# The cubic of a GELU gate: from two GpSimd operations to a scaled square and one VectorE operation

## The chip, the cores and the metric

The kernel runs on one core of a Trainium2 chip. Its time is device microseconds of one launch, and the median of a few runs is compared. The profile is that of one execution, with a clock that starts at its first instruction.

A core has a matrix engine (TensorE, PE), and three engines that work on tiles of 128 partitions: VectorE (DVE), ScalarE (ACT) and GpSimd (POOL). SyncE (SP) issues most of the transfers. Each engine takes its instructions in the order in which they are written, and the engines wait for each other through semaphores.

## The reference

Two layers of a streaming encoder over 16 meta tokens, 1024 prompt tokens and 32 sample tokens, 1024 wide. In each layer a normalised input is multiplied by one combined matrix, whose columns are the low-rank query, the latent of keys and values, the rotary key, the input of a linear recurrence, and the recurrence's gate:

```python
z = rmsnorm(x, norm_mix_g) @ w_in
c_q, c_kv, k_r, x_r, g_r = jnp.split(z, IN_SPLITS, axis=-1)
...
_, h = lax.associative_scan(lru_combine, (a, b), axis=1)
y = h.astype(x.dtype) * jax.nn.gelu(g_r)
```

`jax.nn.gelu` is the tanh form: 0.5 g (1 + tanh(sqrt(2/pi) (g + 0.044715 g^3))). Attention, an output projection and a squared-ReLU MLP follow. Everything is in float32, on 512 gate channels per layer.

## The kernel before, in words

Activations lie transposed: features on the 128 partitions, tokens in the free dimension (1074 columns with two of padding; in the second layer the gate needs only 1056). The 512 channels of recurrence and gate are four tiles, c = 0 to 3, called channels below. All engines' programs are written out by hand in one fixed order each, and all waits are explicit.

**Exact products by splitting.** Every float32 product is three passes on PE: high part times high part, high times low, low times high (`product`, line 975 of the profile; the rotary key's two passes are line 1099). The weights of block b are loaded by SP into `raw_all`, ACT rounds them to `whi` (`split` in ACT's program, L1551), DVE subtracts to give `wlo` (`split` in DVE's, L2294; `split_kr`, L2306, for the rotary key). Both are two buffers deep. ACT's split of block b waits until PE has finished block b-2. PE waits for `w_hi` before the first pass of a product and for `w_lo` before the third; the gates and the rotary-key product wait for `w_lo` at their first.

**PE's order in this stage:** four recurrence inputs, gate products 0 and 1 (blocks 4 and 5), recurrence gates of channel 0 (block 6, a short unit: L1033 and L1036), gate products 2 and 3 (7, 8), recurrence gates 1 (9), latent (CKV) products 0 and 1 (10, 11), recurrence gates 2 (12), rotary key (13), query products 0 and 1 (14, 15), recurrence gates 3 (16), the remaining query products (17 to 20).

**PSUM.** Two slots of three banks hold the products in turn. DVE's `scaled` (L2317) empties a slot into SBUF, multiplied by the inverse root of the mean square. PE reuses a slot only after that.

**The gate's path for channel c.** `gelu_a` on ACT squares `g[c]` into the tile `t2` (L1610, semaphore `g_sq`). `cube` on POOL turns it into the cubic in two operations (L3267 and L3269, semaphore `g_cube`). `gelu_b` on ACT takes the tanh (L1614, `g_tanh`). `gelu` on DVE makes the product with the recurrence's state (L2375, L2376, `y`).

**The recurrence's path.** ACT's `gate_r`, `gate_i`, `decay` and `normal` lead to DVE's `lru` (three operations L2360, L2362, L2363, then the scan L2365). `xc_hi` on ACT and `xc_lo` on DVE make the input of the recurrence gates.

**The orders around the change.** ACT: for channel 0 `normal(0)`, `split(9)`, `gelu_a(0)`, `gelu_b(0)`, `split(10)`, `gate_r(1)`; for channel 1 `normal(1)`, `split(12)`, `gelu_a(1)`, `gelu_b(1)`, `split(13)`, `gate_r(2)`; for channel 2 `gelu_a(2)`, `split(16)`, `gelu_b(2)`, squares of the latent, `split(17)`; for channel 3 `gelu_a(3)`, `split(19)`, inverse root of the latent, `gelu_b(3)`. DVE's order is in the diff.

Of the kernel before, what the change touches and what calls it, by code (L numbers as in the profile page):

```python
# [15 lines left out]
ALU = mybir.AluOpType  # L16
ACT = mybir.ActivationFunctionType
# [19 lines left out]
LAST_KEYS, SAMPLE_KEYS = 8 * P, 9 * P  # L37
assert SAMPLE_KEYS == PAST_A + PAST - 48 and LAST_KEYS + 64 == PAST_A + NMETA and KEY_END == SAMPLE_KEYS + 112
GELU_C = float(np.sqrt(2.0 / np.pi))


B_XR, B_GR, B_CKV, B_KR = [0, 1, 2, 3], [4, 5, 7, 8], [10, 11], 13
# [39 lines left out]
def pairs(name, j):  # L82
    return groups(name, NGROUP) + PAIR[name] * (j - NPAIR + 1) if j else 0
# [334 lines left out]
def trunk(nc, xT, wst, vec, fgain, ropeC, ropeS, ident_in, past_ckv, past_kpe, h0, conv0,  # L418
          yT, ckv_out, kpe_out, h_out, conv_out, x_scr, sum_scr):
    ctx = ExitStack()  # L420
    with ctx:
# [14 lines left out]
        def place(name, region, offset, cols, dt=F32):  # L436
            return nc.alloc_sbuf_tensor_at(name, [P, cols], dt, offset=regions[region] + offset, align_bytes=8)

        def tiles(name, region, first, n, dt=F32):
            return [place(f"{name}{i}", region, (first + i) * TB, T, dt) for i in range(n)]  # L440
# [11 lines left out]
        t1, t2, t3 = (tp[i][:, 0:T] for i in range(3))  # L452
        t4 = tp[3]
        xr = [tp[3], tp[0], tp[1], tp[2]]
        g = tiles("g", "G", 0, 4)
        ckv = [place(f"ckv{i}", "CK", i * KB, KW) for i in range(2)]
        kpe = place("kpe", "KP", 0, KW)
# [85 lines left out]
        def sb(name, shape, dt=F32):  # L543
            return enter(nc.sbuf_tensor(name, shape, dt))
# [4 lines left out]
        sp2, spw = sb("sp2", [P, 4]), sb("spw", [P, 16])  # L549
# [17 lines left out]
        def sem(name, per_layer=0):  # L567
            s = enter(nc.semaphore(name))
            PER[name] = per_layer
            S[name] = s  # L570

        S = {}
        for name, per in (
            ("dve_chain", DVE_CHAIN), *ALL_RAW.items(), ("w_hi", B_MLP), ("w_lo", B_MLP), ("mm", NU),
            ("sum", 6), ("vec_in", 16), ("small_in", 48), ("table_in", 32), ("const_in", 0), ("const_set", 0), ("head_in", 0), ("head", 0), ("ones_set", 0),
            *((f"x_in{m}", 32) for m in range(8)), ("x_out", 32 * 8), *((f"staged{i}", 0) for i in range(N_STAGE)), ("xg_hi", 8), ("xg_lo", 8), ("sq", 8), ("sq_sum", 7),
            ("root", 6), ("rstd", 6), ("sum_hi", 4), ("sum_lo", 4),
            ("xr_ev", 4), ("xr_raw", 0), ("conv", 4), ("xc_hi", 4), ("xc_lo", 4),
            ("gate_r", 4), ("gate_y", 4), ("gate_t", 4), ("gate_i", 4), ("root_t", 4), ("hid", 4),
            ("gr_ev", 4), ("g_sq", 4), ("g_cube", 4), ("g_tanh", 4), ("y", 4),  # L580
            ("ckv_ev", 2), ("ckv_sq", 2), ("ckv_sum", 1), ("ckv_n", 2), ("ckv_hi", 2), ("ckv_lo", 2),
            ("kr_lo", 1), ("kr_ev", 1), ("kpe", 16 * 4), ("kpe_copy", 1), ("kpe_ones", 1), ("kv_out", 32), ("ckv_full", 1), ("hid_out", 1), ("small_out", 48), ("g_poly", 4), ("spw_abs", 1), ("spw_exp", 1), ("sp2", 1),
            ("cq_ev", 6), ("cq_sq", 6), ("cq_sum", 5), ("cq_hi", 6), ("cq_lo", 6),
            ("qr_raw", 2), ("qn", 4), ("qr", 2), ("ra0", 16 * 4), ("ra1", 16 * 4),
            ("y_sq", 4), ("y_sum", 3), ("y_n", 4), ("v_one", 1), ("v_ev", 10), ("kf", 4),
            ("kslot_hi", 3), ("kslot_lo", 4),
            ("slot1_set", 2 + NH // 2 - 1), ("p_zero", 5), ("qn_hi", NH), ("q_hi", NH), ("k_hi", NH), ("q_lo", NH), ("s", NH * NP), ("p", NH * NP),
            ("pv", NH * NP), ("mxmm", NH * NMX), ("mxred", NH * NMX), ("mxc", NH), ("mxt", NH), ("mt_hi", NH), ("mt_lo", NH),
            ("aug", 32 * NH), ("aug_few", 32 * NH), ("o_ev", 3 * NH), ("s_ev", 3 * NH), ("sum_out", 16 * NH), ("sum_in", 16 * 4), ("inv", 4), ("inv_out", 16 * 4),
            ("inv_in", 16 * NH), ("o", 4), ("o_sq", 4), ("o_sum", 3), ("o_hi", 4), ("o_lo", 4),  # L590
            ("y_hi", 4), ("y_lo", 4), ("oy_ev", 8), ("oo_ev", 8), ("xm_f", len(F_ORDER)), ("xm_hi", 24), ("xm_lo", 24), ("xm_sq", 8), ("xm_sum", 7),
            *((name, pairs(name, NPAIR)) for name in ("draw0", "draw1", "s_made", "u_sum", "u_hi", "u_lo", "up", "p_copy", "c_add", "down", "d_add",
                                                      "relu", "f_sq", "f_hi", "f_lo", "prod", "t_made", "x_copy", "x_add", "d_sum")), ("res_add", 8),
            ("end_sq", 0), ("end_sum", 0), ("end_log", 0), ("end_rs", 0),
            ("yout", 0), ("y_st", 0),
        ):
            sem(name, per)
# [913 lines left out]
        def _(act):  # L1511
# [29 lines left out]
            for L in range(DEPTH):  # L1541
                def w(name, k):
                    assert k > 0, name
                    act.wait_ge(S[name], L * PER[name] + k)
# [10 lines left out]
                def live(tile):  # L1555

                    return tile[:, LIVE[0]:LIVE[1]]
# [48 lines left out]
                def gelu_a(c):  # L1606
                    w("gr_ev", c + 1)
                    if c:
                        w("y", c)
                    nc.scalar.activation(live(t2), live(g[c]), ACT.Square).then_inc(S["g_sq"], 1)  # L1610

                def gelu_b(c):
                    w("g_cube", c + 1)
                    nc.scalar.activation(live(t2), live(t2), ACT.Tanh, scale=GELU_C).then_inc(S["g_tanh"], 1)  # L1614

# [209 lines left out]
                for gi in range(NH * NP):  # L1825
# [20 lines left out]
                    if h == NH - 1 and i in Y_AT:  # L1846
                        c = Y_AT.index(i)
# [376 lines left out]
        def _(dve):  # L2224
            V = nc.vector
# [38 lines left out]
            for m in range(8):  # L2264
                dve.wait_ge(S["xg_hi"], m + 1)
                V.scalar_tensor_tensor(out=xgl[m][:, :], in0=x[m], scalar=col(V_GMIX + m), in1=xgh[m][:, :].bitcast(F32),
                                       op0=ALU.mult, op1=ALU.subtract).then_inc(S["xg_lo"], 1)
# [9 lines left out]
            for L in range(DEPTH):  # L2277
# [12 lines left out]
                def split(b):  # L2290

                    w("w_hi", b + 1)
                    n = WCOLS[b]
                    V.tensor_tensor(wlo[b % 2][:, 0:n], raw[b % 2][:, 0:n], whi[b % 2][:, 0:n].bitcast(F32), ALU.subtract).then_inc(S["w_lo"], 1)  # L2294
# [7 lines left out]
                def split_kr():  # L2302

                    w("w_hi", B_KR + 1)
                    hi, src = (t[B_KR % 2][:, :].rearrange("p (k n) -> p k n", k=8)[:, :, 64:P] for t in (whi, raw))
                    V.tensor_tensor(hi, src, hi.bitcast(F32), ALU.subtract).then_inc(S["w_lo"], 1)  # L2306
# [7 lines left out]
                def scaled(u, dst, by, name, at=(0, T)):  # L2314

                    w("mm", u + 1)
                    V.tensor_tensor(chunks(dst, at), slot(u, at), chunks(by, at), ALU.mult).then_inc(S[name], 1)  # L2317
# [38 lines left out]
                def lru(c):  # L2356
# [12 lines left out]
                    V.tensor_copy(hbuf[:, c, 0:1], xc[c][:, STREAM - 1:STREAM])  # L2369
                    link(V.tensor_copy(hbuf[:, c, 1:2], xc[c][:, TOK - 1:TOK]))  # L2370

                def gelu(c):

                    w("g_tanh", c + 1)
                    link(V.scalar_tensor_tensor(out=live(g[c]), in0=live(t2), scalar=1.0, in1=live(g[c]), op0=ALU.add, op1=ALU.mult))  # L2375
                    V.scalar_tensor_tensor(out=live(g[c]), in0=live(g[c]), scalar=0.5, in1=live(xc[c]), op0=ALU.mult, op1=ALU.mult)\  # L2376
                        .then_inc(S["y"], 1)
# [77 lines left out]
                lru(0)  # L2455
                split(9)
                scaled(U_GR[3], g[3], rs, "gr_ev", LIVE)
                split(10)
                gelu(0)
                xc_lo(2)  # L2460
# [2 lines left out]
                lru(1)  # L2463
                split(12)
                scaled(U_CKV[1], ckv[1][:, 0:T], rs, "ckv_ev")
                split_kr()
                gelu(1)
                split(14)
# [4 lines left out]
                split(15)  # L2473
                lru(2)
                split(16)
                scaled(U_CQ[0], cq[0], rs, "cq_ev", LIVE)
                gelu(2)
                scaled(U_CQ[1], cq[1], rs, "cq_ev", LIVE)
# [4 lines left out]
                lru(3)  # L2483
                w("root", SUM_KV)
                scaled(U_CQ[2], cq[2], rs, "cq_ev", LIVE)
                split(19)
                gelu(3)
                V.tensor_copy(hbuf[:, 3, 1:2], xc[3][:, TOK - 1:TOK]).then_inc(S["hid_out"], 1)
# [183 lines left out]
                for h in range(NH):  # L2672
                    for i in range(NP):
# [21 lines left out]
                        if h == NH - 1 and i in Y_AT:  # L2695
                            c = Y_AT.index(i)
# [542 lines left out]
        def _(pool):  # L3239
            G = nc.gpsimd  # L3240
# [4 lines left out]
            for L in range(DEPTH):  # L3245
                def w(name, k):
                    assert k > 0, name
                    pool.wait_ge(S[name], L * PER[name] + k)
# [11 lines left out]
                def live(tile):  # L3260

                    return tile[:, LIVE[0]:LIVE[1]]

                def cube(c):

                    w("g_sq", c + 1)
                    G.tensor_scalar(live(t2), live(t2), 0.044715, 1.0, ALU.mult, ALU.add).then_inc(S["g_poly"], 1)  # L3267
                    w("g_poly", c + 1)
                    G.tensor_tensor(live(t2), live(t2), live(g[c]), ALU.mult).then_inc(S["g_cube"], 1)  # L3269

                def add(acc, tmp, sq, out, m):

                    w(sq, m + 1)
# [7 lines left out]
                def y_add(m):  # L3281
                    add(live(t3), live(t4), "y_sq", "y_sum", m)

                for c in range(3):
                    cube(c)
                sum_squares(ckv_tmp[0][:, :], ckv_tmp[1][:, :], 2, "ckv_sq", "ckv_sum")
                cube(3)
                y_add(1)
                cq_add(1)
                y_add(2)  # L3290
# [280 lines left out]
```

## Time and profile before

| | |
|---|---|
| median of 3 runs | 2461.35 us (2460.33 to 2462.65) |
| profiled execution, span | 2460.3 us |
| PE, DVE busy | 2447.1, 1782.1 us |
| ACT, POOL busy | 1250.7, 517.4 us |
| stage of the gate, first layer | about 73 to 194 us |
| stage of the gate, second layer | about 1300 to 1420 us |

The page gives the profiled execution's own time as its span alone, from the first to the last instruction; the three timed runs are other executions of the same program. A line of the profile names the engine, the source line and the tiles, with the duration and, in brackets, how long the engine sat idle before and who ended that. Consecutive operations of one engine overlap by about 0.1 us, so start-to-start times are a little shorter than durations.

### The profile page before, as it was taken

To read this page: it belongs to the slowest core of one execution; us is meant where nothing else is said; L and a number is where in the kernel's file an instruction comes from. 1 tells how busy PE (TensorE), PEld (TensorE's weight loads), DVE (VectorE), ACT (ScalarE), POOL (GpSimd) and SP (SyncE) were. 2 spreads that over 40 slices of the span, in tenths; PEclk is the share of its full clock that TensorE was granted. 3 is DMA by queue.
4 is the path that set the end of the run, shared out by engine and by line. 5 is a ranking of instruction groups with operands and counts; after the bars stand their busy time and mean duration, and the time that the engine had idled before them with its cause. 6 is when DMAs were issued, how large, how long until landed. Compare 5 with 4: busy or idle time off the path is not lost.

```text
span 2460.3 us, 43868 instructions
## 1 busy us (share of the span) xinstructions
PE 2447.1 (99%) x17366; PEld 2361.9 (96%) x17366; DVE 1782.1 (72%) x2788; ACT 1250.7 (51%) x2237; POOL 517.4 (21%) x479
## 2 busy tenths in 40 slices
PE   9999999999999999999999999999999999999998
PEld 9999977899999999999999998779999999999998
DVE  8677767578876677677676777674887766776676
ACT  5566355435554454455525663554355544554454
POOL 0024255100112211220201142541001112111212
PEclk9999999999999999999999999999999999999999
DMA  4122201222447634764731222013135456546655
GB/s 164 52 61 73 61 11 38 90 60 102 94 86 141 125 85 99 133 120 90 218 100 52 60 74 61 11 38 98 53 115 108 88 119 132 105 88 122 131 106 181
DMA packets 104873, 230.39 MB, mean 94 GB/s; under 512 B 14896, under 2 KB 18320, under 8 KB 104672
## 3 DMA queue, kind: packets, MB, share of 16 engines
q0 software_dynamic: 43648, 89.14, 20.5%
q1 hardware_dynamic: 60880, 138.42, 17.9%
q8 instruction: 139, 2.28, 0.4%
q14 instruction: 62, 0.51, 0.1%
q10 hardware_dynamic: 144, 0.04, 0.0%
HBM read 144.03 MB, written 81.18 MB: 92 GB/s over the span
## 4 chain that ended last, share of the span: by engine, by line
PE 95%; DVE 2%; DMA 1%; issue 1%; ACT 0%; POOL 0%; SPq 0%; DVEq 0%; POOLq 0%; ACTq 0%
PE ps L975 28%; PE ps L1357 23%; PE ps L1406 22%; PE ps L1221 5%; PE ps L1236 4%; PE ps L1498 3%; PE ps L1291 2%; PE ps L1469 2%; PE ps L1168 2%; PE ps L1193 1%; DMA x_scratch<-stage 1%; PE ps L1099 1%; DVE mxp L2620 0%; DVE xall L2879 0%; PE ps L1004 0%
## 5 line engine op out<-in xcount | busy, mean ns | idle before, releaser
L2910 DVE TENSOR_TENSOR wlo<-raw_all,whi 128x512 fp32r<-128x512 f32 (+1 forms) x420 | 270.6, 653 | 181.3 <-ACT whi L2055 178.7
L2055 ACT ACTIVATE whi<-raw_all 128x512 fp32r<-128x512 f32 (+1 forms) x420 | 248.5, 599 | 275.4 <-PE ps L1357 85.9
L3408 POOL DMA_DIRECT2D x_scratch<-stage x224 | 199.7, 941 | 840.5 <-DVE stage L3053 695.4
L2108 ACT ACTIVATE stage<-ps 128x536 f32<-128x536 f32 (+1 forms) x224 | 135.6, 612 | 152.7 <-PE ps L1406 141.6
L3053 DVE TENSOR_TENSOR stage<-stage,ps 128x536 f32<-128x536 f32 (+1 forms) x168 | 119.0, 708 | 86.2 <-PE ps L1406 84.8
L2620 DVE TENSOR_REDUCE mxp<-ps 64x1 f32<-64x64 f32 (+11 forms) x384 | 140.4, 372 | 55.1 <-PE ps L1168 48.4
L1551 ACT ACTIVATE whi<-raw_all 128x1024 fp32r<-128x1024 f32 (+3 forms) x72 | 66.6, 925 | 199.6 <-PE ps L975 199.3
L975 PE MATMUL ps<-xgh,whi 128*128 128x358 f32 (+1 forms) x720 | 157.2, 327 | 0.0
L975 PE MATMUL ps<-xgl,whi 128*128 128x358 f32 (+1 forms) x720 | 156.7, 326 | 0.0
L975 PE MATMUL ps<-xgh,wlo 128*128 128x358 f32 (+1 forms) x720 | 156.6, 326 | 0.0
L975 PEld LDWEIGHTS ps<-xgl,whi 128*128 128x128 f32 x720 | 124.1, 189 | 0.0
L975 PEld LDWEIGHTS ps<-xgh,whi 128*128 128x128 f32 x720 | 123.6, 189 | 0.2 <-issue 0.2
L975 PEld LDWEIGHTS ps<-xgh,wlo 128*128 128x128 f32 x720 | 123.3, 189 | 0.0
L1221 PE MATMUL ps<-pn,v 128*65 128x320 f32 (+1 forms) x288 | 106.3, 453 | 0.0
L1834 ACT ACTIVATE pn<-ps 128x320 f32<-128x320 f32 (+1 forms) x144 | 65.4, 454 | 71.4 <-PE ps L1236 70.0
L1236 PE MATMUL ps<-qo,koh 128*128 128x320 f32 (+7 forms) x304 | 96.9, 400 | 0.0
L2294 DVE TENSOR_TENSOR wlo<-raw_all,whi 128x1024 fp32r<-128x1024 f32 (+3 forms) x70 | 81.2, 1161 | 21.5 <-ACT whi L1551 20.7
L1236 PE MATMUL ps<-qe,keh 97*128 97x320 f32 (+7 forms) x304 | 95.7, 396 | 0.3 <-issue 0.2
L3043 DVE TENSOR_TENSOR raw_all<-raw_all 128x256 f32<-128x256 f32 x224 | 89.5, 420 | 2.0 <-DMA raw_all<-in_wst 1.0
L1834 ACT ACTIVATE pd<-ps 16x64 f32<-16x64 f32 (+4 forms) x352 | 56.7, 224 | 55.2 <-PE ps L1236 54.9
L3393 POOL DMA_DIRECT2D raw_all<-in_wst x30 | 29.8, 993 | 252.6 <-DMA raw_all<-in_wst 252.6
L1236 PEld LDWEIGHTS ps<-qo,koh 128*128 128x128 f32 x304 | 54.8, 190 | 26.2 <-issue 5.2
(846 smaller groups left out, 7687.7 us busy)
## 6 DMA issues: line engine op xcount, KB each, us to landing
raw_all<-in_wst SPq DMA_DIRECT2D x233, 256.0 KB, 3.3
raw_all<-in_wst SPq DMA_DIRECT2D x78, 512.0 KB, 3.6
x_scratch<-stage POOLq DMA_DIRECT2D x112, 268.0 KB, 6.1
x_scratch<-stage POOLq DMA_DIRECT2D x112, 264.0 KB, 5.9
x_scratch<-xall POOLq DMA_DIRECT2D x24, 537.0 KB, 3.6
xall<-x_scratch SPq DMA_DIRECT2D x24, 537.0 KB, 9.7
xall<-in_xT SPq DMA_DIRECT2D x16, 537.0 KB, 6.4
raw_all<-in_wst POOLq DMA_DIRECT2D x30, 256.0 KB, 5.4
```

The costliest lines, as they stand in the source:

```text
L975: mm = nc.tensor.matmul(dst(q), wt, r(q), start=(k == 0 and i == 0), stop=(k == n - 1 and i == 2))
L1221: mm = nc.tensor.matmul(ps[0:65, bank, c0:c0 + n], v[:, v0:v0 + 65], p_tile(gk)[:, 0:n], start=(k in FIRST), stop=(k in LAST))
L1236: mm = nc.tensor.matmul(ps[:, gi % 3, 0:n], ks[e][0 if a == "h" else 1][rows, k0:k0 + P], qs[e][0 if c == "h" else 1][rows, q0:q0 + n], st ...
L1357: mm = nc.tensor.matmul(ps[:, 2 * slot_ + t, 0:HN], wt, rhs[:, t * HN:(t + 1) * HN], start=(opens and n == 0), stop=(n == 11), skip_group_ ...
L1406: mm = nc.tensor.matmul(ps[:, 2 * slot_ + t, 0:HN], ring(u, whi if a == "h" else wlo)[:, wc], fop[q, f + c][:, t * HN:(t + 1) * HN], start ...
L1834: ins = nc.scalar.activation(dst[r0:r1, c0:c1], src[r0:r1, c0:c1], ACT.Exp, scale=SM_SCALE)
L2055: nc.scalar.activation(dst, src, ACT.Copy).then_inc(S["u_hi"], 1)
L2108: nc.scalar.activation(quarters(stage_of(L, g, i, n)[:, 0:N2]), src, ACT.Copy, scale=-1.0 if row else 1.0).then_inc(S["x_copy"], 1)
L2620: ins = V.reduce_max(mxp[lo_:hi_, tile, part:part + 1], ps[lo_:hi_, max_bank(h, s), c0:c0 + n], AX_X)
L2910: V.tensor_tensor(dst, src, hi.bitcast(F32), ALU.subtract).then_inc(S["u_lo"], 1)
L3053: V.tensor_tensor(st, st, src, op).then_inc(S["x_add"], 1)
L3408: pool.dma_start(x_scr[2 * i + row, :, a:b], stage_of(L, g, i, n)[:, 0:b - a], accum_op=ALU.add).then_inc(S[done], 16)
```

## The change

The factor 0.044715 moves into ACT's square, as its root in the scale. DVE then adds 1 and multiplies by `g[c]` in one operation. POOL's two operations and the semaphore between them go. The new operation stands in DVE's program at four places.

```diff
+GELU_CUBE = float(np.sqrt(0.044715))
...
-                    nc.scalar.activation(live(t2), live(g[c]), ACT.Square).then_inc(S["g_sq"], 1)
+                    nc.scalar.activation(live(t2), live(g[c]), ACT.Square, scale=GELU_CUBE).then_inc(S["g_sq"], 1)
...
+                def cubic(c):
+                    w("g_sq", c + 1)
+                    V.scalar_tensor_tensor(out=live(t2), in0=live(t2), scalar=1.0, in1=live(g[c]), op0=ALU.add, op1=ALU.mult).then_inc(S["g_cube"], 1)
...
                 lru(0)
                 split(9)
                 scaled(U_GR[3], g[3], rs, "gr_ev", LIVE)
+                cubic(0)
                 split(10)
                 gelu(0)
...
                 lru(1)
                 split(12)
                 scaled(U_CKV[1], ckv[1][:, 0:T], rs, "ckv_ev")
+                cubic(1)
                 split_kr()
                 gelu(1)
...
                 lru(2)
                 split(16)
+                cubic(2)
                 scaled(U_CQ[0], cq[0], rs, "cq_ev", LIVE)
                 gelu(2)
...
                 lru(3)
                 w("root", SUM_KV)
                 scaled(U_CQ[2], cq[2], rs, "cq_ev", LIVE)
+                cubic(3)
                 split(19)
                 gelu(3)
...
-                def cube(c):
-                    w("g_sq", c + 1)
-                    G.tensor_scalar(live(t2), live(t2), 0.044715, 1.0, ALU.mult, ALU.add).then_inc(S["g_poly"], 1)
-                    w("g_poly", c + 1)
-                    G.tensor_tensor(live(t2), live(t2), live(g[c]), ALU.mult).then_inc(S["g_cube"], 1)
...
-                for c in range(3):
-                    cube(c)
                 sum_squares(ckv_tmp[0][:, :], ckv_tmp[1][:, :], 2, "ckv_sq", "ckv_sum")
-                cube(3)
                 y_add(1)
```

## Rows read from the trace of the kernel before

**Rows 1.** The page's first part: busy time and share of the span by engine.
```profile
PE 2447.1 (99%) x17366; PEld 2361.9 (96%) x17366; DVE 1782.1 (72%) x2788; ACT 1250.7 (51%) x2237; POOL 517.4 (21%) x479
```

**Rows 2.** Chain of waits, first layer: start us, length us, engine and line.
```profile
105.08 1.16 PE ps L1033 x6
106.23 0.98 PE ps L1036 x6
107.22 23.61 PE ps L975 x144
130.83 0.09 issue
130.92 1.39 PE ps L1033 x6
...
133.29 7.86 PE ps L1099 x48
...
164.76 1.16 PE ps L1033 x6
```

**Rows 3.** Timeline of PE, first layer: start us, length us, operation.
```profile
107.06 0.66 PE L975 MATMUL ps<-xgh,whi 128*128 128x358 f32 x3
...
108.04 0.65 PE L975 MATMUL ps<-xgh,wlo 128*128 128x358 f32 x3
```

**Rows 4.** Timeline of ACT, first layer; in brackets the idle time before it.
```profile
100.30 1.10 ACT L1614 ACTIVATE t<-t 128x1074 f32<-128x1074 f32 x1 [3.00 <-POOL t L3269]
105.17 1.06 ACT L1551 ACTIVATE whi<-raw_all 128x1024 fp32r<-128x1024 f32 x1 [3.77 <-PE ps L975]
...
139.40 2.22 ACT L1571 ACTIVATE xcs<-xc 64x1074 fp32r<-64x1074 f32 x2
...
154.78 1.10 ACT L1614 ACTIVATE t<-t 128x1074 f32<-128x1074 f32 x1
155.79 2.08 ACT L1688 ACTIVATE ckv_tmp<-ckv 128x1074 f32<-128x1074 f32 x2
164.86 1.06 ACT L1551 ACTIVATE whi<-raw_all 128x1024 fp32r<-128x1024 f32 x1 [6.99 <-PE ps L975]
```

**Rows 5.** Timeline of DVE, first layer, same columns.
```profile
96.12 2.20 DVE L2362 SCALAR_TENSOR_TENSOR t<-t,xc 128x1074 f32<-128x1074 f32 x1
98.35 3.05 DVE L2363 SCALAR_TENSOR_TENSOR t<-t,t 128x1074 f32<-128x1074 f32 x1
...
105.12 1.28 DVE L2317 TENSOR_TENSOR g<-ps,rs 128x1074 f32<-128x1074 f32 x1 [0.47 <-PE ps L975]
106.31 1.22 DVE L2294 TENSOR_TENSOR wlo<-raw_all,whi 128x1024 fp32r<-128x1024 f32 x1
...
130.39 0.42 DVE L2294 TENSOR_TENSOR wlo<-raw_all,whi 128x256 fp32r<-128x256 f32 x1
130.87 1.28 DVE L2317 TENSOR_TENSOR ckv<-ps,rs 128x1074 f32<-128x1074 f32 x1
132.06 0.68 DVE L2306 TENSOR_TENSOR whi<-raw_all,whi 128x512 fp32r<-128x512 f32 x1
...
188.68 1.28 DVE L2317 TENSOR_TENSOR cq<-ps,rs 128x1074 f32<-128x1074 f32 x1
```

**Rows 6.** Operations on the gate tiles, both layers: least/median/greatest ns.
```profile
L3269 POOL TENSOR_TENSOR t<-t,g x8: 2945/3178/3410, 97.3 to 1406.9; 128x1074 f32<-128x1074 f32 x4, 128x1056 f32<-128x1056 f32 x4
L2375 DVE SCALAR_TENSOR_TENSOR g<-t,g x8: 1243/1257/1273, 107.4 to 1416.5; 128x1074 f32<-128x1074 f32 x4, 128x1056 f32<-128x1056 f32 x4
```

**Rows 7.** Chain of waits, second layer.
```profile
1330.90 1.20 PE ps L1033 x6
...
1356.69 0.00 issue
```

**Rows 8.** The page's part on DMA issues: KB, us to landing.
```profile
raw_all<-in_wst SPq DMA_DIRECT2D x78, 512.0 KB, 3.6
```

**Rows 9.** Span and mean granted TensorE clock.
```profile
core 0: 2460.3 us, clock 0.999
```

More of the change, by code:

```diff
@@ L581, in trunk @@
             ("ckv_ev", 2), ("ckv_sq", 2), ("ckv_sum", 1), ("ckv_n", 2), ("ckv_hi", 2), ("ckv_lo", 2),
-            ("kr_lo", 1), ("kr_ev", 1), ("kpe", 16 * 4), ("kpe_copy", 1), ("kpe_ones", 1), ("kv_out", 32), ("ckv_full", 1), ("hid_out", 1), ("small_out", 48), ("g_poly", 4), ("spw_abs", 1), ("spw_exp", 1), ("sp2", 1),
+            ("kr_lo", 1), ("kr_ev", 1), ("kpe", 16 * 4), ("kpe_copy", 1), ("kpe_ones", 1), ("kv_out", 32), ("ckv_full", 1), ("hid_out", 1), ("small_out", 48), ("spw_abs", 1), ("spw_exp", 1), ("sp2", 1),
             ("cq_ev", 6), ("cq_sq", 6), ("cq_sum", 5), ("cq_hi", 6), ("cq_lo", 6),
```

## The prediction

> **What bounds the kernel now.** I read the page's busy shares first. TensorE (PE) is busy 2447.1 us of the 2460.3 us span, 99%, with VectorE (DVE) at 72%, ScalarE (ACT) at 51% and GpSimd (POOL) at 21% [rows 1]. On such a kernel work taken off POOL buys nothing by itself. What counts is whether PE ever waits because of an edit. The chain of waits says how close that is in the stage of the change: from 105.08 to 164.76 us it is PE from one group to the next, and the only piece in it that is not PE is 0.09 us at 130.83 [rows 2]. So almost no PE waiting can be removed there, and any lateness that reaches PE is paid in full, since nothing later has slack to give back.
>
> What PE needs at each boundary stands in the code: the rounded weights of its block (semaphore `w_hi`, ACT's split), their remainders (`w_lo`, DVE's split), and the PSUM slot emptied. Weight buffers are two deep, so ACT's split of block b may begin only when PE has finished block b-2. A short PE unit, the gates, covers that split.
>
> **The change, part by part.** Removed: eight POOL pairs, four per layer. A product took 2.95 to 3.41 us [rows 6]. POOL's last product of a channel ended just before ACT's tanh: the tanh started at 100.30 us after 3.00 us of waiting for POOL [rows 4]. Added: eight DVE operations of 128x1074 or 128x1056. Their nearest row is the first operation of the gate's product, the same opcode with the same two inputs: 1.24 to 1.27 us [rows 6]. I take 1.27 and 1.25. It can't be much else: same bytes, same buffers. The factor in ACT's square: the tanh with a factor takes 1.10 us [rows 4]; I take no change, within 0.02 us, and ACT is idle for microseconds around it in channels 0 to 2.
>
> What is moved matters more. The cubic now stands in DVE's order, and for channels 0 and 1 it stands behind an evacuation of PSUM that waits for PE. Behind the cubic waits ACT's tanh, and behind the tanh on ACT stands the split that PE needs next.
>
> *Channel 0, first layer.* DVE's evacuation of the last gate product starts at 105.12, 0.04 us after PE ends it at 105.08 [rows 2, 5]. The next DVE operation starts 1.19 us later, at 106.31 [rows 5]; that is now the cubic, to 107.59. Until then the tanh, which ran at 100.30, can't start. It runs at 107.62 (0.03 us from one engine to the other, as at 100.30), and the next ACT operation follows 1.01 us later (154.78 to 155.79 [rows 4]): split 10 at 108.63, taking 1.06 us [rows 4], to 109.69. Before, it ran at 105.17 to 106.23 and PE came for it at 107.06 [rows 3, 4]: a delay of 3.46 us against 0.83 of cover. PE's handover from DVE took 0.11 us (remainders ready 130.39 + 0.42, matmul at 130.92) [rows 2, 5], so PE starts at 109.80 instead of 107.06: 2.74 us. Then its third pass, 0.98 us after the first [rows 3], needs the remainders too: DVE's split 10 runs 109.72 to 110.95 (1.23 with 0.03 of handover), PE goes on at 111.06 instead of 108.04. **Loss at this place: 3.0 us.**
>
> *Channel 1, first layer.* Both the end of the second latent (CKV) product and all that waits for it move by 3.0, from 130.83 to 133.83. The gates of channel 2 no longer wait at their start: the recurrence before split 12 on DVE gets faster, because its slowed operations (2.20 us at 96.12 and 3.05 at 98.35 in channel 0, against 1.27 for such an operation elsewhere [rows 5, 6]) ran while POOL was working on its product. Unheld, they would start one row's overlap earlier, which gives back 0.25 us: 133.67. They take 2.14 us (1.16 + 0.98) [rows 2], so PE wants the rotary-key product at 135.81. DVE: evacuation at 133.87, cubic at 135.06 to 136.34. ACT: tanh 136.37, split 13 at 137.38 to 138.44. DVE: the subtraction of this block, 0.68 us [rows 5], 138.47 to 139.15. PE: 139.26 instead of 135.81. **Loss: 3.45 us.** It is larger than the first since PE waits for the remainders from the first matmul of this product.
>
> Here a rule of the Trainium skill bears on a step. The row shows 2.20 and 3.05 us where 1.27 is usual, only beside POOL's product [rows 5]. The GPSIMD Engine Reference (section 8, Key points) says that GpSimd shares its memory interfaces with the vector engine and contends with vector operations that read two inputs. By it DVE gets some 2.7 us back per channel and the 0.25 us above is gained; if the slowness had another cause and stayed, split 12 on DVE would end about when PE wants it, and the first layer's 0.25 and the second's 0.15 would be lost: 12.8 us in place of 12.4.
>
> *Channel 2.* The cubic stands after split 16 and before the evacuation. The tanh started at 154.78, 13.6 us after the rotary-key product's end at 141.15 [rows 2, 4]; it now starts some 16.1 after it; the two squares of the latent and POOL's sum move with it by 2.6. The next thing PE wants of ACT is split 17, which waits 6.99 us for PE anyway [rows 4]. Nothing reaches PE.
> *ACT's backlog in between.* After the second stop ACT's high parts for channel 3 (139.40, 2.22 us) [rows 4] move by about 4.9 us, to 146.5, with PE's product ending at 147.2. Still in time.
> *Channel 3.* The evacuation ran at 188.68 [rows 5]; without POOL the recurrence ends 3.0 us earlier, so the cubic ends about 188.2, the tanh 189.3, and DVE's split 19 keeps its place. Nothing reaches PE, a little is gained for later work that is not late.
> *DMA.* A raw block is reloaded after DVE's split; it lands in 3.6 us [rows 8] and is wanted some 10 us later. No queue of SP or POOL is passed in a way that matters: POOL's own later sums only come sooner.
>
> *Second layer.* The same order, with 1056 columns in the gate tiles. PE ends the last gate product at 1330.90 and the CKV product at 1356.69 [rows 7]. With 1.25 for the cubic: first place 2.9, given back 0.15, second place 3.4. Sum 6.2.
>
> Sum: 3.0 - 0.25 + 3.45 = 6.2 in the first layer, 6.2 in the second, 12.4 us. The profiled execution had a span of 2460.3; the three runs lie between 2460.33 and 2462.65, median 2461.35, so about 1 us lies around the span and the shift applies to the median as it is: **2473.7 us**, 0.5% slower. Cost bounds: each of the four stops holds cubic (1.19 to 1.31), tanh (1.0 to 1.1), and handovers that I know to 0.1; four times +-0.3 gives +-1.2.
>
> **Rivals.**
> A, both stops paid: 2473.7.
> B, *only the first is paid*. After it, DVE and ACT are ahead of PE, and if that lead carried over, the second stop would vanish: 2461.35 + 5.9 - 0.4 = 2466.9. For it: the recurrence is 3 us shorter. Against: evacuation and cubic of channel 1 hang on PE's own end, which no lead moves.
> C, *the array's clock falls*. Now it is granted 0.999 of full, the 2.4 GHz level, over the whole span [rows 9], with PE never idle longer than at its start. Two of the new stops leave PE idle 3.3 us (gates over at 133.83 + 2.14, start at 139.26). If the clock went to 1.2 GHz after these and stayed there for the rotary-key product of 7.86 us [rows 2], each would add 7.9: 2489. In the Trainium skill, TensorE: Matmul & The Clock Gate (HAM oscillation) warns of just such idle stretches between bursts. No row of this case shows one.
> D, *not slower*. PE could have slack that the profile doesn't show: its ends are modelled, and if the tanh and split 10 landed within it, only the two small waits at the gates of channel 2 would go, 0.09 and its overlap per layer, thanks to POOL's silence: 2461.0. It decides only if the cubic of channel 0 came before the evacuation of the last gate product, that is 2.7 us earlier than the order says. The wait in the code stands against it.
> E, *a third stop*: channel 2's late tanh, or ACT's backlog for channel 3 with its 0.7 us of slack, reaches PE. Up to 1.5 us per layer: 2476.7.
>
> **How the numbers follow.** A 79%, B 5%, C 7%, D 4%, E 5%. A's own range is 2472.5 to 2474.9. To leave out no more than 2 in 10 and take in the model's errors, B's edge and E, the range is 2468 to 2480. A difference under 0.2%, 4.9 us, can't be told from none. A, C, E and B (by 5.5 us) are over it, D is not: 0.96 slower, of which B's nearness to the bound takes 0.02, so 0.94, the same 0.05, faster 0.01.
>
> **What would show it.** Right, if the new profile has in each layer two PE idle stretches of about 2.7 and 3.4 us in L975 and L1099, ended by the split of ACT and of DVE, if the tanh of channels 0 and 1 waits for a DVE operation of 1.25 us and starts 2.5 us after PE's product ends, and if the recurrence's three operations all take 1.3 us. Wrong in the first place, if PE starts the product after the gates of channel 1 within 1 us of their end; wrong in the second, if the rotary-key product follows the gates at once; wrong in the terms, if a cubic takes 2 us or more; and C would show as a granted clock below 1 in the window after a stop.

## The result, and the profile after

The changed kernel takes 2478.07 us (median of 5, 2476.48 to 2480.65) where the kernel before takes 2460.33 us beside it (2458.92 to 2462.65): ratio 1.0073, 95% interval 1.0062 to 1.0084. It is 17.7 us slower. The forecast was 12.4 us slower.

The profiled execution has a span of 2476.3 us, 16.0 more than before. Its list of what PE waited for, longest first (engine and line, the releaser, us in total, times, longest), begins with two entries that the kernel before did not have:

```profile
PE ps L1100 <- DVE whi L2307: 6.4, 2, 3.2
PE ps L976 <- ACT whi L1552: 4.9, 2, 2.5
```

L976 is the product (L975 before), L1100 the rotary-key product, L1552 ACT's split, L2307 DVE's subtraction for the rotary key. So there are four stops of PE, two per layer, 11.3 us in all. The other entries are under 1 us each, but for one of 1.3 that both kernels have.

The chain of waits in the first layer shows how each arises. It answers to [rows 2], where the chain never left PE:

```profile
105.25 1.28 DVE g L2318
106.53 1.20 DVE t L2376
...
107.75 0.02 ACT t L1615
...
108.75 1.05 ACT whi L1552
...
109.84 25.21 PE ps L976 x144
...
135.08 1.28 DVE ckv L2318
136.36 1.20 DVE t L2376
...
138.58 1.05 ACT whi L1552
...
139.65 0.70 DVE whi L2307
...
140.40 9.53 PE ps L1100 x48
149.93 23.61 PE ps L976 x144
```

PE's end releases DVE's evacuation (L2318). The cubic (L2376) follows, then ACT's tanh (L1615), then the split (L1552), then PE. In the second stop DVE's subtraction stands between split and PE. Before, the tanh stood nowhere on the path. The same rows on ACT and DVE, to be held against [rows 4, 5], where the tanh waited 3.00 us for POOL and was over well before PE's end:

```profile
107.75 1.10 ACT L1615 ACTIVATE t<-t 128x1074 f32<-128x1074 f32 x1 [10.31 <-DVE t L2376]
```

```profile
96.26 1.28 DVE L2363 SCALAR_TENSOR_TENSOR t<-t,xc 128x1074 f32<-128x1074 f32 x1
97.57 1.28 DVE L2364 SCALAR_TENSOR_TENSOR t<-t,t 128x1074 f32<-128x1074 f32 x1
...
105.25 1.28 DVE L2318 TENSOR_TENSOR g<-ps,rs 128x1074 f32<-128x1074 f32 x1 [3.16 <-PE ps L976]
106.45 1.27 DVE L2376 SCALAR_TENSOR_TENSOR t<-t,g 128x1074 f32<-128x1074 f32 x1
```

The tanh now waits 10.31 us for DVE. The cubic takes 1.27 us, as taken from [rows 6], and the recurrence's two operations at 96.26 and 97.57 take 1.28 us each where [rows 5] has 2.20 and 3.05.

The PE timeline behind the first stop shows what the forecast lacked. Each row is one pass of three matmuls, and the column to read is the start:

```profile
109.84 1.26 PE L976 MATMUL ps<-xgh,whi 128*128 128x358 f32 x3 [2.50 <-ACT whi L1552]
110.91 1.09 PE L976 MATMUL ps<-xgl,whi 128*128 128x358 f32 x3
111.80 1.09 PE L976 MATMUL ps<-xgh,wlo 128*128 128x358 f32 x3
112.69 0.70 PE L976 MATMUL ps<-xgh,whi 128*128 128x358 f32 x3
113.23 0.66 PE L976 MATMUL ps<-xgl,whi 128*128 128x358 f32 x3
```

From 109.84 the passes start 1.07, 0.89 and 0.89 us apart. In [rows 3] two passes take 0.98 us together. From 113.23 the pace is 0.49 again. The windows of this stretch show what went with it; the column behind POOL is the granted TensorE clock:

```profile
core 0: us, PE busy (x) PEld busy (x) DVE busy (x) ACT busy (x) POOL busy (x), PEclk, DMA share, GB/s
...
108.00:110.00 2.00, 0.16 (x1) 0.16 (x1) 0.18 (x1) 2.00 (x3) 0.00 (x0) 0.84 0.00 0
110.00:112.00 2.00, 2.00 (x7) 2.00 (x8) 2.00 (x2) 1.99 (x3) 0.00 (x0) 0.50 0.00 0
112.00:114.00 2.00, 2.00 (x11) 2.00 (x11) 1.52 (x2) 1.96 (x4) 0.00 (x0) 0.81 0.86 240
114.00:116.00 2.00, 2.00 (x14) 2.00 (x13) 0.00 (x0) 1.96 (x3) 0.00 (x0) 1.00 0.06 23
```

The array's clock fell from full to half, the 1.2 GHz level, during the stop, stayed there into the window from 112 us, and was back at 2.4 GHz by 114. The Trainium skill (TensorE: Matmul & The Clock Gate, HAM oscillation) says that idle gaps between bursts of matmuls send the array back to its low clock, so that the next burst starts cold; the trace agrees, with 0.50 from 110 to 112 us. It happened behind all four stops of this execution, but not behind every such stop: the experiment with the filled stops has a second execution of the changed kernel where it did not happen behind the first. The rotary-key product behind the second stop fills 9.53 us, from 140.40 to 149.93, against 7.86 in [rows 2].

Two marks add the losses up. The rotary-key product ended at 141.15 (133.29 + 7.86) [rows 2] and ends at 149.93 now: 8.78 us later, 0.15 of which was there before the first stop (105.08 [rows 2], 105.23 now). In the second layer the gate product ends at 1339.89, 8.99 later than the 1330.90 of [rows 7], and the first query product begins at 1384.85; the rows are the evacuation behind the one and the start of the other:

```profile
1339.92 1.26 DVE g L2318
...
1384.85 23.42 PE ps L976 x144
```

In the chain of the kernel before the same query product began at 1366.93:

```profile
1366.93 23.42 PE ps L975 x144
```

That is 17.92 us later, 8.93 of them lost in this stage. The two stages lose 8.63 + 8.93 = 17.6 us, and the medians differ by 17.7.

### The profile page after: what moved, and what is told of

It reads as the page before. It is cut to its first block, busy times and chain, and to the rows that moved or that the text cites. A ratio compares the mean times of both kernels' runs of the same rounds, so it can differ in the third digit from the quotient of the medians.

```text
span 2476.3 us, 43860 instructions
## 1 busy us (share of the span) xinstructions
PE 2452.0 (99%) x17366; PEld 2367.5 (96%) x17366; DVE 1765.8 (71%) x2796; ACT 1250.5 (50%) x2237; POOL 484.0 (20%) x463
## 3 DMA queue, kind: packets, MB, share of 16 engines
q1 hardware_dynamic: 60880, 138.42, 17.6%
## 4 chain that ended last, share of the span: by engine, by line
PE 94%; DVE 3%; DMA 1%; issue 1%; ACT 1%; POOL 0%; SPq 0%; DVEq 0%; ACTq 0%; POOLq 0%
PE ps L976 27%; PE ps L1358 23%; PE ps L1407 23%; PE ps L1222 5%; PE ps L1237 5%; PE ps L1499 3%; PE ps L1292 2%; PE ps L1169 2%; PE ps L1470 1%; PE ps L1100 1%; PE ps L1194 1%; DMA x_scratch<-stage 1%; DVE xall L2889 0%; PE ps L1005 0%; DVE msq L2247 0%
## 5 line engine op out<-in xcount | busy, mean ns | idle before, releaser
L976 PE MATMUL ps<-xgh,whi 128*128 128x358 f32 (+1 forms) x720 | 158.4, 328 | 4.9 <-ACT whi L1552 4.9
L1552 ACT ACTIVATE whi<-raw_all 128x1024 fp32r<-128x1024 f32 (+3 forms) x72 | 66.6, 925 | 184.7 <-PE ps L976 184.4
L976 PE MATMUL ps<-xgl,whi 128*128 128x358 f32 (+1 forms) x720 | 157.7, 327 | 0.0
L976 PE MATMUL ps<-xgh,wlo 128*128 128x358 f32 (+1 forms) x720 | 157.4, 327 | 0.0
L976 PEld LDWEIGHTS ps<-xgh,whi 128*128 128x128 f32 x720 | 124.3, 190 | 5.7 <-ACT whi L1552 5.5
L976 PEld LDWEIGHTS ps<-xgl,whi 128*128 128x128 f32 x720 | 125.2, 191 | 0.0
L976 PEld LDWEIGHTS ps<-xgh,wlo 128*128 128x128 f32 x720 | 124.1, 190 | 0.0
L1237 PEld LDWEIGHTS ps<-qe,keh 97*128 97x128 f32 x304 | 54.6, 190 | 26.4 <-issue 7.9
```

The costliest lines, as they stand in the source:

```text
L976: mm = nc.tensor.matmul(dst(q), wt, r(q), start=(k == 0 and i == 0), stop=(k == n - 1 and i == 2))
L1237: mm = nc.tensor.matmul(ps[:, gi % 3, 0:n], ks[e][0 if a == "h" else 1][rows, k0:k0 + P], qs[e][0 if c == "h" else 1][rows, q0:q0 + n], st ...
```

## The experiments

All but one, which is the changed kernel itself, are edits of it. Each was timed against the kernel before on one chip. Where the texts say "my theory", it is this: a cubic costs nothing by itself; behind a PSUM evacuation it makes ACT's tanh, and the split behind that, late; and the array's clock falls after each stop and adds to its price.

**Both cubics ahead of the evacuation.**

```diff
-                scaled(U_GR[3], g[3], rs, "gr_ev", LIVE)
                 cubic(0)
+                scaled(U_GR[3], g[3], rs, "gr_ev", LIVE)
...
-                scaled(U_CKV[1], ckv[1][:, 0:T], rs, "ckv_ev")
                 cubic(1)
+                scaled(U_CKV[1], ckv[1][:, 0:T], rs, "ckv_ev")
```

> The cubics of channels 0 and 1 stand ahead of the PSUM evacuation instead of behind it; nothing else differs from the changed kernel. My theory (the loss is only the place in DVE's order, which makes ACT's tanh and the split behind it late): both stops vanish in both layers, PE is not idle between the gates and the next product, the granted clock stays at 0.999, and the 0.2 to 0.3 us that PE waited at the gates of channel 2 go too. Time 2459.9 us where the kernel before has 2460.3, ratio 0.9998 (0.999 to 1.001). Rival (a cubic on DVE costs something by itself, through memory traffic or DVE's load): the ratio stays at 1.002 or more.

Measured: 2459.86 us (2458.06 to 2460.4) against 2460.31, ratio 0.9997 (0.9988 to 1.0006). In DVE's timeline, then ACT's, the cubic runs at 101.98 while DVE would be idle, and the tanh is over by 104.39. The split (L1552) waits 0.89 us for PE again, as it should:

```profile
101.98 1.27 DVE L2376 SCALAR_TENSOR_TENSOR t<-t,g 128x1074 f32<-128x1074 f32 x1
105.22 1.28 DVE L2318 TENSOR_TENSOR g<-ps,rs 128x1074 f32<-128x1074 f32 x1 [1.97 <-PE ps L976]
```

```profile
103.29 1.10 ACT L1615 ACTIVATE t<-t 128x1074 f32<-128x1074 f32 x1 [5.88 <-DVE t L2376]
105.28 1.06 ACT L1552 ACTIVATE whi<-raw_all 128x1024 fp32r<-128x1024 f32 x1 [0.89 <-PE ps L976]
```

The whole loss is gone, and neither entry is left in the list of PE's waits. It was the cubic's place in the order, not the operation. The interval includes 1, so this kernel is not shown to beat the one before. The 0.4 us that it might gain at the gates of channel 2 are below what can be told.

**One at a time.** Only the first of the two edits above, then only the second.

> Only channel 0's cubic is moved ahead of the evacuation; channel 1's stays behind it. My theory: one stop per layer is left, before the rotary-key product. It costs 3.4 us of idle PE and about 1.5 us of a lower array clock after it, less 0.25 us at the gates of channel 2: 2 x 4.6 = 9.3 us, ratio 1.0038. Rival (the second stop is a consequence of the first, as a backlog of ACT): the second goes with the first, ratio 1.000.

> Only channel 1's cubic is moved ahead of the evacuation; channel 0's stays behind it. My theory: the stop before the first CKV product is left, 2.7 us of idle PE and 1.4 us after it, less 0.3 us: 2 x 3.8 = 7.5 us, ratio 1.0031. With the other single move the two losses add up to the changed kernel's 1.0070 to 1.0073. Rival (each stop's price depends on the other): the two don't add up within 0.0010.

Measured, with only channel 0's cubic early: 2469.86 us, ratio 1.0039 (1.0026 to 1.0052). With only channel 1's: 2468.29 us, ratio 1.0032 (1.0021 to 1.0042). The list of PE's waits has one of the two new entries in each, word for word as it stands above: L1100's alone with channel 0's cubic early, L976's alone with channel 1's. So each stop idles PE as long alone as together with the other.

0.0039 and 0.0032 add up to 0.0071, against 0.0073 and 0.0071 for both (the two measurements of the changed kernel). Within intervals of 0.0010 to 0.0015 to either side the stops are independent. Neither hangs on the other, which also answers rival B's idea of a lead carried over.

**The factor alone.** POOL keeps both operations; the factor stands in ACT's square.

```diff
+                def cube(c):
+                    w("g_sq", c + 1)
+                    G.tensor_scalar(live(t2), live(t2), 1.0, 1.0, ALU.mult, ALU.add).then_inc(S["g_poly"], 1)
+                    w("g_poly", c + 1)
+                    G.tensor_tensor(live(t2), live(t2), live(g[c]), ALU.mult).then_inc(S["g_cube"], 1)
...
+                for c in range(3):
+                    cube(c)
                 sum_squares(ckv_tmp[0][:, :], ckv_tmp[1][:, :], 2, "ckv_sq", "ckv_sum")
+                cube(3)
...
-                cubic(0)
...
-                cubic(3)
```

> The factor stands in the scale of ACT's square, but POOL still adds one and multiplies in its two operations, where it did before. My theory: the scaled square takes 1.08 to 1.10 us like the plain one, nothing moves, ratio 1.0000 (0.9990 to 1.0010). Rival (a scale costs ACT time): the square is longer by some 0.1 us, but with ACT idle after it the ratio would still be 1.000, so the row and not the ratio decides.

Measured: 2459.80 us, ratio 0.9999 (0.9989 to 1.0008). The group of the square, in ns (least, median, greatest), was 1072/1080/1092 before and is now:

```profile
L1611 ACT ACTIVATE t<-g x8: 1072/1082/1090, 94.9 to 1404.9; 128x1074 f32<-128x1074 f32 x4, 128x1056 f32<-128x1056 f32 x4
```

The scale in the square costs nothing that shows.

**The stops filled with work.** This kernel adds matmuls whose results are overwritten by the product behind them.

```diff
+                FILL = (15, 18)
+                def keep_busy(u, n):
+                    for i in range(n):
+                        nc.tensor.matmul(ps[:, 3 * slot_of(u) + i % 3, 0:CH], ones_r[:, :], xgh[0][:, 0:CH], start=True, stop=True)
...
+                    if u == U_CKV[0]:
+                        take(u)
+                        keep_busy(u, FILL[0])
                     w("w_hi", b + 1)
...
-                    w("w_lo", B_KR + 2)
                     take(U_KR)
+                    keep_busy(U_KR, FILL[1])
+                    w("w_lo", B_KR + 2)
```

> The changed kernel, with matmuls whose result is overwritten put into the two stops of each layer: 15 of 358 columns before the first CKV product and 18 before the rotary-key product, once the PSUM slot is free and before the wait for the weights. They keep PE active, and make nothing arrive sooner. My theory (5 of the 17.7 us are the array's clock, which falls to 1.2 GHz after each stop): the granted clock stays at 0.999, the passes after the stops take 0.49 us from start to start, and the time is the stops alone, 12.4 us over the kernel before, ratio 1.0050 (1.0045 to 1.0058). Rival (the slow passes come from refilling or from waiting for remainders): ratio 1.0070 as for the changed kernel.

> The changed kernel once more, on the same chip and beside the same runs as the kernel with filled stops: ratio 1.0073 (1.0062 to 1.0084) by either theory.

Measured: with the stops filled 2472.53 us (2471.16 to 2473.80), ratio 1.0047 (1.0034 to 1.0061); the changed kernel once more 2478.72 us (2474.55 to 2480.32), ratio 1.0071 (1.0056 to 1.0087). The intervals of the ratios overlap a little, the two sets of times do not. The PE timeline of the filled kernel around the first stop, around the second, and its windows behind each (L987 is its product, L1112 its rotary-key product, L967 the filler):

```profile
107.25 2.60 PE L967 MATMUL ps<-xgh,ones_r 128*128 128x358 f32 x15
109.91 0.76 PE L987 MATMUL ps<-xgh,whi 128*128 128x358 f32 x3
110.50 0.65 PE L987 MATMUL ps<-xgl,whi 128*128 128x358 f32 x3
111.17 0.76 PE L987 MATMUL ps<-xgh,wlo 128*128 128x358 f32 x3
```

```profile
136.04 3.08 PE L967 MATMUL ps<-xgh,ones_r 128*128 128x358 f32 x18
139.43 0.76 PE L1112 MATMUL ps<-xgh,whi 128*128 128x358 f32 x3 [0.31 <-DVE whi L2319]
```

```profile
110.00:112.00 2.00, 1.99 (x11) 1.69 (x12) 2.00 (x2) 1.99 (x3) 0.00 (x0) 1.00 0.00 0
...
140.00:142.00 2.00, 2.00 (x14) 2.00 (x13) 1.84 (x2) 1.98 (x2) 0.00 (x0) 1.00 0.74 203
```

The product starts at 109.91, no sooner than without the filler, so the stop is as long as before. But the next two passes start 0.59 and 0.67 us apart, not 0.89 and more, and the granted clock stays at 1.00. The third pass (111.17) comes 1.26 us after the first, and the forecast, which has it wait for the remainders, puts 1.26 between them. The rotary-key product begins at 139.43; the forecast had 139.26. The filled kernel is 12.0 us over the kernel before, as the stops alone would be. The other 5 to 6 us are the clock's. Its chain has the same marks as above, the start of the query product in each layer and the end of the second layer's gate product:

```profile
147.59 23.61 PE ps L987 x144
...
1337.12 1.16 PE ps L1045 x6
...
1379.34 23.42 PE ps L987 x144
```

The first layer's mark is 6.44 us later than before, 0.21 of which was there before the stop (its gates of channel 1 begin at 105.29); in the second layer 6.22 us turn into 12.41. So the stages lose 6.23 and 6.19 us, 12.4 in all, where the changed kernel lost 17.6.

The second execution of the changed kernel adds something that the first did not show. Its stops are as long (2.50 us idle before 109.74), but behind the first one the clock did not fall. The product in its chain, in two pieces, and the window:

```profile
109.74 1.24 PE ps L976 x6
...
111.00 22.91 PE ps L976 x138
```

```profile
110.00:112.00 2.00, 1.98 (x12) 1.69 (x12) 2.00 (x2) 1.99 (x3) 0.00 (x0) 1.00 0.00 0
```

From its start to its end at 133.92 the product takes 24.2 us, as in the filled kernel (109.91 to 134.08), against 25.2 in the first execution: the same kernel and the same stop, and 1.0 us less with the clock kept. With only channel 1's cubic early the clock fell late: the first two passes behind the stop in the first layer were still 0.60 and 0.66 us apart, and it stood at 0.88 from 110 to 112 us and at 0.50 from 112 to 114. Over the four profiles (the changed kernel twice, and one cubic early at a time) it fell behind 11 of 12 stops, and the product behind took 1.0 to 1.5 us longer than in the filled kernel. What decides whether it falls is not shown.

**ACT's split ahead of the tanh.** DVE's order is left as changed.

```diff
-                gelu_b(0)
                 split(10)
+                gelu_b(0)
...
-                gelu_b(1)
                 split(13)
+                gelu_b(1)
```

> The changed kernel with ACT's split 10 ahead of the tanh of channel 0, and split 13 ahead of that of channel 1. DVE's order stays, so the remainders of these blocks still come behind the cubic, 1.2 us late. My theory: ACT's part of the loss goes. PE waits 0.9 us before the third pass of the first CKV product and 1.1 us before the rotary-key product. Per layer 0.9 + 1.1 - 0.25 = 1.75, both 3.5 us, ratio 1.0014, if a stop of 1 us leaves the clock alone; 1.0038 if it falls for as long as after the stops of 3 us. Rival (the loss is DVE's alone): ratio at 1.0070.

Measured: 2463.85 us, ratio 1.0014 (1.0005 to 1.0023). PE's waits, the passes around the first stop, and the windows with the two stops:

```profile
PE ps L1100 <- DVE whi L2307: 2.0, 2, 1.0
...
PE ps L976 <- DVE wlo L2295: 1.1, 2, 0.6
```

```profile
107.68 0.65 PE L976 MATMUL ps<-xgl,whi 128*128 128x358 f32 x3
108.89 0.75 PE L976 MATMUL ps<-xgh,wlo 128*128 128x358 f32 x3 [0.57 <-DVE wlo L2295]
```

```profile
108.00:110.00 2.00, 1.43 (x10) 1.15 (x9) 1.97 (x2) 2.00 (x3) 0.00 (x0) 1.00 0.05 12
...
134.00:136.00 2.00, 1.05 (x6) 1.06 (x7) 1.43 (x3) 1.92 (x3) 0.00 (x0) 1.00 0.00 0
```

What is left is the part that goes through DVE alone: the third pass starts 1.21 us after the second where 0.49 is usual, and the rotary-key product is held for 1.0. About four fifths of the loss (0.0058 of some 0.0072) went through ACT, the clock's share with it, where the rival put it all on DVE. The two stops that are left, 0.6 and 1.0 us of idle PE, left the clock at 1.00 in both layers.

**POOL for channels 0 and 1, DVE for 2 and 3.** POOL's `cube` as in the experiment on the factor, but called for two channels, and `cubic(0)` and `cubic(1)` left out.

```diff
-                cubic(0)
...
-                cubic(1)
...
+                for c in range(2):
+                    cube(c)
                 sum_squares(ckv_tmp[0][:, :], ckv_tmp[1][:, :], 2, "ckv_sq", "ckv_sum")
```

> POOL makes the cubic of channels 0 and 1 as in the kernel before, with the factor in ACT's square; DVE makes those of channels 2 and 3 where the change puts them. My theory (channels 2 and 3 cost nothing): ratio 1.0000 (0.9990 to 1.0010), no idle time of PE in the stage beyond the 0.1 us at the gates of channel 2. Rival (channel 2's tanh, 2.5 us later, reaches PE over the latent's squares or the recurrence gates of channel 3): ratio 1.0010 or more, with a wait in front of the gates of channel 3 or of the sum of squares.

Measured: 2459.53 us, ratio 0.9998 (0.9989 to 1.0008). Channels 2 and 3 cost nothing that can be told. This kernel also holds both sides of the contention in one execution. The two recurrence operations (L2363 and L2364) in DVE's timeline of channel 1, with POOL at work (its addition from 121.88, its product from 123.06 to 126.47), and of channel 2, with POOL idle:

```profile
121.90 2.19 DVE L2363 SCALAR_TENSOR_TENSOR t<-t,xc 128x1074 f32<-128x1074 f32 x1
124.13 3.47 DVE L2364 SCALAR_TENSOR_TENSOR t<-t,t 128x1074 f32<-128x1074 f32 x1
```

```profile
150.16 1.28 DVE L2363 SCALAR_TENSOR_TENSOR t<-t,xc 128x1074 f32<-128x1074 f32 x1
151.47 1.28 DVE L2364 SCALAR_TENSOR_TENSOR t<-t,t 128x1074 f32<-128x1074 f32 x1
```

## Why the prediction was right, and where it was short

- *PE has no slack, so lateness is paid in full*: right. The stages' loss of 17.6 us is the difference of the medians, 17.7.
- *Channel 0's stop, 2.74 us to the first pass*: 2.78 by the clock of the trace (107.06 to 109.84), 2.63 after taking off the 0.15 that was there before. The chain through evacuation, cubic, tanh and split ran as laid out, each step within 0.15 us.
- *Channel 1's stop, 3.45 us*: 3.4. The filled kernel put the product's start within 0.17 us of the forecast.
- *What is given back at the gates of channel 2*: right. The recurrence is as fast as forecast without POOL, and the two early cubics leave no wait there. Its worth, 0.4 us, can't be told from noise.
- *Channels 2 and 3, the factor, DMA*: no cost, shown by the kernels with the last two channels, with the factor alone, and with both cubics early.
- *Sum*: 12.4 us against 17.7. With the clock kept up the filled kernel's two stages lose 6.2 us each, as forecast A adds them up. The mis-sized term is the one taken as zero in A and priced in rival C: the array's clock. It was given 7% and 7.9 us after each of two stops, and measured at 1.0, 1.4, 1.2 and 1.5 us after the four, 5.2 in all (the changed kernel's products behind the stops against the filled kernel's). 12.4 and 5.2 are 17.6. The mechanism of C was right in kind, and the sign that the prediction gave for it, a granted clock below 1 behind a stop, was seen. It was wrong in two respects: the stops of 2.5 us brought it on too, and it lasted some 3 us and not the length of a product.
- *Rivals B, D and E* did not happen. B and D fell with the changed kernel's own trace, where both stops stand in each layer. E fell with the kernel of the last two channels, and for ACT's backlog with the chain of the changed kernel, which is PE alone behind the second stop.

That the range held the time is in part luck. It was drawn to take in B's edge, E and the errors of A; C, the rival whose mechanism moved the time, stood at 2489 and outside it. A's own range, 2472.5 to 2474.9, did not hold the time, and the kernel in which the clock is kept up lies at its edge, at 2472.53.

The prediction also read one thing wrong without harm to the shift: it puts about 1 us between a span and its time. In the runs whose span is on record it is about 1.8. By that the profiled execution of the kernel before, with its span of 2460.3, took some 2462.1 us (an estimate), 1.7 above the median of 2460.33, while the changed kernel's is its median. This is why the spans differ by 16.0 us and the medians by 17.7.

One thing stays open. From the start of the second layer's queries to the end, the ten profiles take between 1091.0 and 1093.4 us. The kernel before is at the upper end, with 1093.4, and the changed one took 1091.5. So single executions move by 2 us outside the stage, for reasons that no kernel here was made to find; the medians are what the comparison rests on.

## What to carry to other kernels

Before moving an operation to another engine, ask what stands in front of it there and what stands behind its consumer. Here an operation of 1.27 us on VectorE, twice per layer, was free in one place and cost 17.7 us in all one line further down, since the line between them waits for the matrix engine itself, and the matrix engine's next weights stood behind the consumer. And price a stop of the matrix engine at more than its length: add what the clock may take after it, here 1.0 to 1.5 us each.

## What was not expected of the hardware

- After an idle stretch of 2.4 to 3.2 us of the matrix engine the granted clock was 0.50 for some 3 us of matmuls, in 11 of 12 cases, and a pass took 0.89 us from start to start in place of 0.49. It cost 1.0 to 1.5 us each time. The twelfth, of 2.50 us, left it at 1.00. So did 0.6 and 1.0 us of idling. Filling the stretch with matmuls on overwritten PSUM kept it at 1.00, and won back 5 to 6 us of a loss whose waits stayed as they were.
- On VectorE two operations of the recurrence took 2.19 and 3.47 us with GpSimd's addition and product running and 1.28 us each without, in one execution. That GpSimd contends with two-input vector operations stands in the Trainium skill (GPSIMD Engine Reference, section 8, Key points), and the trace agrees. Here such an operation took up to 2.7 times as long (3.47 against 1.28); the rows of the kernel before had 2.4 times (3.05).
